# Moving the stage buffers of a two-block transformer kernel 160 bytes up in SBUF

## What is computed

```python
def swiglu(x, w_gate, w_up, w_down):
    return (jax.nn.silu(x @ w_gate) * (x @ w_up)) @ w_down        # 1024 -> 2816 -> 1024

# block one
x = layer_norm(alpha * x + 0.5 * swiglu(x, ...))                  # FFN 0
x = layer_norm(alpha * x + hybrid_mixer(x, ...))                  # three attentions, 3 branch products, w_out
x = layer_norm(alpha * x + 0.5 * swiglu(x, ...))                  # FFN 1
# block two: gated delta rule + block-sparse attention, gates, w_o, per-layer embedding,
# then a GEGLU FFN with a width-3 causal convolution (FFN 2) and a final gate product
```

## Time and profile before

| | |
|---|---|
| median of 3 runs (range) | 1124.57 us (1124.35 to 1125.56) |
| span of the profiled execution | 1122.6 us |
| TensorE matmul busy | 1094.1 us, 97% |
| TensorE weight load busy | 1023.2 us, 91% |
| GpSimd busy | 902.3 us, 80% |
| ScalarE busy | 621.2 us, 55% |
| VectorE busy | 495.1 us, 44% |
| granted TensorE clock, mean | 0.998 |

### The profile page before, as it was taken

How to read it: one execution, slowest core, us unless ns; L and a number is a source line. 1 busy time by engine, 2 the same in 40 slices (tenths; PEclk the granted TensorE clock), 3 DMA queues, 4 the chain that set the end, 5 groups by cost and what they waited for, 6 DMA issues and landing times.

```text
span 1122.6 us, 22288 instructions
## 1 busy us (share of the span) xinstructions
PE 1094.1 (97%) x8110; PEld 1023.2 (91%) x8110; DVE 495.1 (44%) x904; ACT 621.2 (55%) x1002; POOL 902.3 (80%) x695
## 2 busy tenths in 40 slices
PE   8999999999999999999999999999999999999997
PEld 7999998999998998999999899889999798999985
DVE  4422113202456554421126655774766256454463
ACT  4444444654667866544443775555666565555564
POOL 6999996898664596999999589577355898999985
PEclk9999999999999999999999999999999999999999
DMA  7866665666342454766665466335233565666652
GB/s 244 282 204 193 187 195 165 206 222 192 115 131 78 130 184 139 230 202 198 192 182 181 135 193 188 118 116 159 65 94 127 183 202 172 180 197 187 189 184 77
DMA packets 52774, 191.29 MB, mean 170 GB/s; under 512 B 5856, under 2 KB 6112, under 8 KB 52320
## 3 DMA queue, kind: packets, MB, share of 16 engines
q1 hardware_dynamic: 50688, 182.47, 52.6%
q10 hardware_dynamic: 2016, 7.81, 2.1%
HBM read 189.21 MB, written 1.05 MB: 169 GB/s over the span
## 4 chain that ended last, share of the span: by engine, by line
POOL 51%; issue 27%; PE 19%; ACT 1%; POOLq 1%; DVE 1%; DMA 1%; SPq 0%; DVEq 0%; ACTq 0%
POOL weights_low L533 51%; PE banks L575 10%; PE acc L575 8%; DMA ring<-in_stream 1%; POOLq L539 0%; ACT weights_high L1440 0%; POOLq L530 0%; ACT tmp L1686 0%; ACT tmp L1956 0%; PE acc L749 0%; PE banks L766 0%; DVE act_buf L2016 0%; DVE res L2162 0%; POOL stat L547 0%; DVE xs L2174 0%
## 5 line engine op out<-in xcount | busy, mean ns | idle before, releaser
L533 POOL TENSOR_TENSOR weights_low<-ring,weights_high 128x512 fp32r<-128x512 f32 x686 | 899.2, 1345 | 208.7 <-ACT weights_high L1440 206.5
L1440 ACT CAST weights_high<-ring 128x1024 fp32r<-128x1024 f32 x343 | 356.1, 1047 | 216.4 <-PE banks L575 132.0
L575 PE MATMUL banks<-xT_high,weights_high 128*128 128x256 f32 x1264 | 351.5, 278 | 1.2 <-POOL weights_low L533 1.1
L575 PE MATMUL banks<-xT_low,weights_high 128*128 128x256 f32 x1264 | 350.3, 277 | 0.0
L575 PE MATMUL banks<-xT_high,weights_low 128*128 128x256 f32 x1264 | 350.3, 277 | 0.0
L575 PEld LDWEIGHTS banks<-xT_high,weights_high 128*128 128x128 f32 x1264 | 237.4, 188 | 4.2 <-issue 1.5
L575 PEld LDWEIGHTS banks<-xT_low,weights_high 128*128 128x128 f32 x1264 | 237.7, 188 | 2.3
L575 PEld LDWEIGHTS banks<-xT_high,weights_low 128*128 128x128 f32 x1264 | 237.9, 188 | 0.0
L1991 DVE TENSOR_TENSOR hf<-act_buf,banks 128x256 f32<-128x256 f32 x40 | 16.8, 421 | 225.2 <-ACT act_buf L1466 211.0
L575 PE MATMUL acc<-xT_high,weights_high 128*128 128x256 f32 x408 | 108.8, 287 | 1.8 <-ACT xT_high L1539 1.0
L575 PE MATMUL acc<-weights_high,hT_high 128*128 128x512 f32 x264 | 104.0, 394 | 2.2 <-issue 1.6
(11 more groups left out here) (362 smaller groups left out, 1577.5 us busy)
## 6 DMA issues: line engine op xcount, KB each, us to landing
ring<-in_stream SPq DMA_DIRECT2D x343, 512.0 KB, 3.7
rows<-in_big_rows ACTq DMA_DIRECT2D x3, 1024.0 KB, 8.2
rows<-in_big_rows ACTq DMA_DIRECT2D x3, 512.0 KB, 4.0
cst<-in_consts ACTq DMA_DIRECT2D x3, 470.5 KB, 4.8
xs<-in_x_tm ACTq DMA_DIRECT2D x2, 512.0 KB, 7.3
out<-xs SPq DMA_DIRECT2D x4, 256.0 KB, 2.1
gates<-in_x_fm SPq DMA_DIRECT2D x2, 256.0 KB, 4.2
ring<-in_stream SPq DMA_DIRECT2D x2, 256.0 KB, 4.3
```

Of the source, the lines that this page charges most:

```text
L533: last = nc.gpsimd.tensor_tensor(wlo[:, slot, hs], ring[:, slot, hs], whi[:, slot, hs].bitcast(F32), ALU.subtract)
L575: ins = nc.tensor.matmul(o, lhsT, rhs, start=start, stop=stop, **kw)
L1440: nc.scalar.copy(whi[:, ch % RING, :], ring[:, ch % RING, :]).then_inc(S["hi_ready"], 1)
```

## The change

`fill_stage` grows by 40 float32 per partition, 160 bytes. No instruction is added, removed, or reordered. Every tensor behind it begins 160 bytes higher: `hT`, `mT`, `oT`, `yT`, `pE` and `rcs` at 192 modulo 1024 (second half 704) where they were at 32. `weights`, `xT`, `ring`, `res`, `xs`, `rows`, `cst` and `tmp` stay. The last tensor still ends within the partition.

```diff
@@ -340,7 +340,7 @@
         nmx2 = sb("nmx2", [2, 4])
         den2 = sb("den2", [2, 4])
         coef2 = sb("coef2", [2, 4])
-        sb("fill_stage", [144])
+        sb("fill_stage", [184])
         hT = pair("hT", [GROUP, T], in_ffn)
         hf = sb("hf", [2, T], in_ffn)
         act_buf = sb("act_buf", [2, 2 * T], in_ffn)
```

## The result

The changed kernel takes 1130.03 us (median of 5 runs, 1129.21 to 1130.75), the kernel before, run beside it, 1125.29 (5 runs, 1124.35 to 1125.56): a ratio of 1.0043 (1.0032 to 1.0053). It is 4.7 us slower where 5.0 us less was forecast. The profiled execution has a span of 1128.1 us against 1122.6.

A forecast was written before the change was run, and what follows sets the result against it. The prediction took TensorE's matmul pitch to bound the FFN loops; 3.3 + 0.9 + 0.8 = 5.0 us less took the span from 1122.6 to 1117.6, giving a time of 1119.6 us, range for 8 in 10 1116.3 to 1129.0.

The forecast's parts named there:

- Term 1: 792 matmuls with hT stationary: 229.1 in place of 233.3 ns each, 3.3 us less.
- Term 2: 192 matmuls with mT and 24 with pE, at the price of xT stationary: 0.9 us less.
- The missing row: The trace has no fp32r operand exactly 64 bytes above a moving weight block; bounds 225 to 237.5 ns a matmul.
- Term 3: 408 matmuls with oT and yT moving: 1.7 us less to 0.2 us more possible, hidden behind GpSimd, taken as nothing.
- Term 4: xT stretches behind 54 down calls find back to the fast rhythm sooner: up to 1.6 us less, 0.8 taken.
- the first rival: FFN loops: xT stretches fall into the 117.8 ns rhythm, 0.20 us each, 1131 us if all 54; chance 0.22.
- partial catch: Case of the first rival: 25 to 45 FFN stretches in the slow rhythm, 1125.4 to 1129.4 us.
- Term 5: All else that moves (attention, delta rule, ScalarE's and VectorE's operands): nothing, with +-0.5 us.
- the second rival: FFN matmuls: 64 above a block costs what 96 below did; time same, 1124.6 (1123.5 to 1125.5); chance 0.20.

The follow-up runs named there:

- the kernel with all at 64: Fill 32 bytes longer than in the kernel before, so hT, mT, oT and yT begin at 64 modulo 1024: 1125.18 us, ratio 1.0001.
- the 16-column matmul: Changed kernel plus one matmul of 16 columns, its output overwritten, between each down and the xT stretch behind it: 1128.85 us, ratio 1.0041.
- the mixed rings: Kernel before with hT's four tiles at differing addresses: 32/64/96/128 1127.35 us; 160/192/224/256 1128.39 us; 128 three times and 32 1128.07 us; 64 three times and 32 1124.34 us.

## Why the prediction was wrong

**The steps that failed** are two. The first is the one behind terms 1 and 2: "operands that begin 64 bytes from a weight block (`xT`) run faster than those that begin 96 bytes from one". That holds 64 bytes below a block, and the kernel with all at 64 shows it: 230.0 ns, and 12 in 2.75 to 2.77 us. 64 bytes above it doesn't hold. With `hT` at 192 the twelve take 2.79 and 2.80 us, 233.0 ns a matmul against the 229.1 that I took. The missing row was named as the one unknown, and its two bounds were right (225 to 237.5); the choice inside them was not. Twelve take, by the start of the tile modulo 512: 2.80 or 2.81 us at 32, 2.75 to 2.77 at 64, 2.80 at 96, 2.72 at 128, 2.79 to 2.81 at 160, 192 and 224, 2.77 to 2.78 at 256. Neither the distance from the weights nor divisibility by 64 orders these.

**Term 1** was forecast at 3.3 us less and came to 792 x 0.3 ns = 0.2 us by the pitch in the loops, 0.7 us by the sum over all 792. **Term 2** was 0.9 us less and came to nothing. In the changed kernel `mT`'s 399 ns members are gone, and yet its pitch is (438.6 - 430.9) / 33 = 233.3 ns, what it was. Line L575, 431 to 441 us, against the earlier trace rows:

```profile
L575 PE MATMUL acc<-weights_high,mT_high x12: 394/394/394, 430.6 to 438.3; 128*128 128x512 f32 x12
L575 PE MATMUL acc<-weights_low,mT_high x12: 394/394/394, 430.9 to 438.6; 128*128 128x512 f32 x12
...
L575 PE MATMUL acc<-weights_high,mT_low x12: 394/394/397, 431.6 to 438.8; 128*128 128x512 f32 x12
```

So the argument from the longest member, 399 against 388, told nothing of the price at a new address. The durations themselves aren't at fault. Member by member, a 512-column matmul here is recorded some 162 ns longer than the distance to the next start: with `mT` before, 394, 399 and 392 go with distances of 232, 237 and 231 ns, and in the changed kernel 394 goes with 233 each time. The three together are what costs: means of 395.0 and 394.0 ns for `mT` before and after, against 391.3 with `xT` stationary. When the longest of three goes and the others rise, nothing is gained.

**Term 3**, nothing for `oT` and `yT`, held: in the timeline `oT` starts at 404.75 and, 39 matmuls on, at 409.34 us, 117.7 ns apiece where it was 117.2.

**Term 4** is the second step that failed, and the larger: it put the hand-over at a gain, and it had the wrong sign. It was to be 0.8 us less for finding back to the quick rhythm. The quick stretches did gain their hundredth (5.46 in place of 5.47), and the other 27 never found back: 5.1 us more. Together the stretches came to 4.8 us more, 5.6 us off the forecast. Of the 10.5 us by which the span was missed (1117.6 against 1128.1), that is the largest part; terms 1 and 2 missed by 3.5 us, and everything outside the loops by 1.4. This is the first rival's mechanism and its price of 0.20 us a stretch. It went to 27 stretches, inside the 25 to 45 of its partial catch. The time, 1130.0, is nevertheless above that case's 1125.4 to 1129.4, since the case took terms 1 and 2 as earned. Without them it reads 1124.6 + 27 x 0.20 = 1130.0. The rival got 0.22 because of two sentences. "All loop periods recover within some five matmuls" was a property of `hT` at 32, one address that sets the quick rhythm from any entry, and I read it as a property of TensorE. "A run should leave TensorE at the moment at which it took it" holds, by the rhythm that follows, at 64 and 160, and fails at 32, 96, 128, 192, 224 and 256.

**Term 5**, nothing for everything else, held by the medians: moving all but `hT` gave 1.0004. In the one profile of the changed kernel the matmuls and stages outside the loops add 1.4 us, more than the 0.5 us that the term allowed. One run of 288 matmuls with `xT`, at 207.5 us, whose addresses didn't change, turned slow as a whole for 1.3 us more; others became quicker or waited longer.

**No dependence on the address**, the second rival, is excluded: between 32 and 96, both on 16-byte lines, lie 9.1 us. The Trainium skill (SBUF — State Buffer, section "SBUF: two separate sides") has TensorE never wait on anyone within the engine side; this kernel's spread of 0.8%, by nothing but where one operand of the matmuls begins, doesn't agree with a matmul that is blind to its operands' place. The runs don't show who the other party is.

**What stays open.** That the rhythm of a stretch isn't fixed by its own addresses, and depends on what ran ahead of it, was shown by intervention (the 16-column matmul) and by the mixed rings. That it is the moment of entry by which this works is argued. Why an address turns one rhythm into another was not found: the map 32 to quick, 96 and 128 to slow, 64 and 160 kept, 192, 224 and 256 exchanged is a list of what was measured. It holds, in one profiled execution of each kernel, for every `down` that stands between two stretches. It doesn't hold for the two `down` calls in a row with which an FFN starts: in the changed kernel they turn slow into quick in FFN 0 and quick into slow in FFN 1, where two exchanges would give back what came in. That TensorE's reads of the stationary and of the moving operand meet on something that repeats by address is argued, not shown.

The sums over the loops close. At 128 the 54 stretches take 9.9 us more than before and all 792 matmuls with `hT` 5.3 us less, from start to start in the traces: 1124.6 + 4.6 = 1129.2 against 1129.3 measured. At 96 they take 10.0 more and 0.8 less: 1133.8 against 1133.65. The forecast for 128 had 1131.2 for the case with every stretch slow; half of its excess comes from 54 x 0.08, which counts 648 of the 792 matmuls. What everything outside the loops adds, between 0.9 us less and 2.8 us more in the traces, differs from kernel to kernel, and one profile of each doesn't say how much of it belongs to the kernel and how much to the execution.

## What to carry to other kernels

Where TensorE runs without a gap, a change of addresses alone can move the time, here by up to 0.8%, by the rhythm in which it leaves the following matmuls more than by the matmuls that read the moved operand. Compare the same stretch of unchanged matmuls in both traces, by the distance of starts, before believing in the effect of any small edit: some of it may be this. A price taken at one distance from a block says nothing of the same distance on the other side; a one-line fill is cheap to try. An address that sets the quick rhythm from either entry is the safe choice: the cheaper one that merely keeps it (64, ratio 1.0001) gave its gain back in the loops that were entered slow, and the cheapest (128, ratio 1.0047) lost.

## What the runs showed of the hardware that was not expected

- fp32r matmuls of 256 columns have two steady rhythms, 113.3 and 117.8 ns, at identical addresses and a granted clock of 0.995 to 0.998 in the profiled runs of both sorts. Once a stretch is in one of them, behind its first five matmuls or so, it keeps it to its end, over all 48 matmuls here.
- 512-column fp32r matmuls take 227 ns with the stationary operand at the weights' own place modulo 512, 229 to 231 at 64 bytes below it (with one run of 24 at 233.5), 231 to 232 at 256 and some 233 at the other places. That is 11 to 17 ns above the 216 ns that the Trainium skill (TensorE: Matmul & The Clock Gate, section "Back-to-back issue gap") gives for an isolated matmul of 512 columns. The one at the weights' own place is the quickest and still gives a slower kernel, ratio 1.0047.
- Splitting one of twelve 512-column matmuls into two of 256 with the same stationary operand costs 0.01 us at most (2.79 and 2.81 us for the 13, 2.79 and 2.80 for the 12).
